# Fox attention: sums turned before they are inverted, raw output turned a unit later, copies begun at another unit

## The chip, the cores and the metric

One NeuronCore of a Trainium2 chip runs the whole program. The metric is the device time of one execution in microseconds (us), lower is better. Only one of the program's stages is touched by the change.

## What is computed

One layer of a hybrid decoder over a prompt of 2048 tokens and 8 sequences of 8 new tokens, all in float32: an input projection, two kinds of attention (8 heads each), an output projection and a squared-ReLU MLP. The stage that the change touches is the prompt's part of the first kind, the forgetting attention ("fox"):

```python
def block(args):                      # one block of 128 queries, 8 heads of 64 dims
    s = einsum('bqhd,bkhd->bhqk', qi, k) * scale
    s = s + ci[..., :, None] - c_k[..., None, :]     # c: running sum of log-forget values
    s = where(kpos[None, :] <= qpos[:, None], s, NEG_INF)
    p = softmax(s, axis=-1)
    return einsum('bhqk,bkhd->bqhd', p, v)
```

A further output of the layer is the window buffer of 8 decode sequences (new_win_k): the old buffer (win_k) shifted by 8 rows. It needs no arithmetic and is copied from memory to memory by DMA while the fox stage runs.

## The kernel before

The program is a row of phases with a barrier of all engines between them: projection, fox attention, dilated attention, the decode samples, and the output projection with the MLP in two halves. `attend_fox` is one phase.

**Tiling.** Heads go in four pairs (p); the 2048 queries in four macros (m) of 512 columns. A *unit* G is two key tiles of 128 keys against one macro, for both heads z of the pair: four score tiles of 128 keys x 512 queries. Causality gives macro m 2(m+1) units, so 20 units a pair (u counts them: 0-1, 2-5, 6-11, 12-19) and 80 in all. `last_unit(n)` is the last unit of macro n = 4p + m (u = 1, 5, 11, 19), and `ended(G - k)` names the macro, if any, that ended k units ago.

**The work of one unit.**
- TensorE writes the transposed scores into one of three PSUM banks `s_ps` (`scores`, L1153, L1154, the mask L1156 on the diagonal). ScalarE turns each into exponentials `pT` in SBUF (L1043); `pT` has room for four units. TensorE multiplies `pT` by the values into `o_ps` (`values`, L1170), for two units at a time, in odd G. GpSimd adds the exponentials up over the key tiles in `acc` (L1002, L1006).
- Beside this, for macros and head pairs that come later, TensorE computes the plain scores once more into one of two PSUM banks `low_ps` (`low_scores`, L1123, L1126), and VectorE takes each row's maximum with the decay added (`largest`, L1062). These "lows" give the number that is subtracted in the softmax. `fox_plan` spreads them over the units, some four to seven in most; after unit 9 of the last pair there are none left. TensorE may start low number o only when VectorE has finished low o - 2: there are two banks.
- When a macro's maxima are there, TensorE transposes them (`turn_max`, L1133) into the shared PSUM bank `x_ps`, and VectorE copies them into `qb` (`take_off`, L1075). This falls in units u = 1, 5, 11 of pair 0, and u = 14, 17 (for the next pair), 4 and 11 after that.

**The end of a macro.** Two units after its last one, TensorE sums `acc` over the partitions with a matrix of ones, so that every one of a head's 64 rows of `x_ps` holds the same sum (`denominators`, L1179). VectorE inverts all 128 x 512 of them and multiplies `o_ps` by the result into `o_f` (`post`, L1082 and L1086). Three units after, TensorE transposes `o_f` into `x_ps` (`turn_back`, L1186), ScalarE copies that into `o_sb` (L1019) and sends it to memory (L1023).

**What sets the order.** Each engine runs its own list in program order: an instruction that waits holds up all that stand behind it. `x_ps` is one bank with several users; `x_uses` lists them in TensorE's order, and `take_x` makes TensorE wait until the one before has been read. In a step G TensorE does: scores with the lows between them, values (odd G), denominators, turn_max, turn_back. VectorE does: lows, post, take_off. ScalarE does: at u = 0 and 10 the issue of a copy of 4080 KB for new_win_k (L1032; eight in all, for G = 0, 10, ... 70), the four exponentials, then fetch_back.

**Loads.** SyncE's queue loads the first pair's data quarter by quarter (x = 0 to 3): q (three DMAs of 256 KB, L898, L899), ka (two, L908), decay (one of 512 KB, L922), kb (one, L912), v (two of 128 KB, L917). The first low needs q and ka of x = 0, VectorE's part of it the decay, the first score kb as well. The loads for the next pair follow through the stage, behind waits on `scored`, `maxed` and `pv`; the last of them, q of macro 3, is issued when unit 19's scores are done and is first needed by the lows of u = 3.

Of the kernel before, what the change touches and what calls it, by code (L numbers as in the profile page):

```python
# [13 lines left out]
ALU = mybir.AluOpType  # L14
# [4 lines left out]
P = 128  # L19
# [6 lines left out]
HD = 64  # L26
# [752 lines left out]
def attend_fox(nc, c, dram):  # L779
# [10 lines left out]
    with Phase(nc, "fox") as ph:  # L790
# [11 lines left out]
        neg_c = ph.sb("neg_c", [P, TILES, HEADS])  # L802
        rden = ph.sb("rden", [P, Q_COLS])
        o_f = ph.sb("o_f", [P, 2, Q_COLS])
# [26 lines left out]
        added = ph.sem("added")  # L831
        den_done = ph.sem("den_done")
        inverted = ph.sem("inverted")
        posted = ph.sem("posted")
        o_turned = ph.sem("o_turned")
        returned = ph.sem("returned")
        o_sent = ph.sems("o_sent")
# [15 lines left out]
        def ended(G):  # L853

            return [n for n in range(HEAD_PAIRS * MACROS) if last_unit(n) == G]
# [15 lines left out]
        def x_uses():  # L871

            uses, count = [], dict(den=0, turn=0, back=0)
            def use(kind):
                count[kind] += 1
                uses.append((kind, count[kind]))
            use("turn")
            for G in range(UNITS + 3):
                for _n in ended(G - 2):
                    use("den")  # L880
                for _x in planned(G, "turn"):
                    use("turn")
                for _n in ended(G - 3):
                    use("back")
            return uses
# [5 lines left out]
        def _(sp):  # L891
# [42 lines left out]

            for x in range(MACROS):
                load_q(0, x)
                load_ka(0, x)
                load_decay(0, x)
                load_kb(0, x)
                load_v(0, x)  # L940
            sp.dma_start(table[:, :], dram["page_table"]).then_inc(table_loaded, 16)
# [72 lines left out]
        def _(act):  # L1014
            def fetch_back(n):
                act.wait_ge(o_turned, n + 1)
                if n >= 2:
                    act.wait_ge(o_sent[n % 2], 16 * (n // 2))
                act.activation(o_sb[:, n % 2, :, :], x_ps[:, :].rearrange("p (j d) -> p j d", d=P), ACT.Copy)\  # L1019
                    .then_inc(returned, 1)  # L1020
                act.wait_ge(returned, n + 1)
                p, m = divmod(n, MACROS)
                act.dma_start(dram["att"][m * Q_COLS:(m + 1) * Q_COLS, p * P:(p + 1) * P]  # L1023
                              .rearrange("(j p) d -> p j d", p=P), o_sb[:, n % 2, :, :]).then_inc(o_sent[n % 2], 16)

            act.wait_ge(decay_set, 1)
            for G in range(UNITS + 3):
                if G < UNITS:
                    p, u, m, kt = unit(G)
                    if u % 10 == 0:  # L1030
                        b = G // 10
# [6 lines left out]
                    for k in range(2):  # L1038
                        x = reach(kt + k, m)
                        for z in range(2):  # L1040
# [3 lines left out]
                                           bias=neg_c[:, kt + k, 2 * p + z:2 * p + z + 1]).then_inc(exped, 1)  # L1044
                for n in ended(G - 3):
                    fetch_back(n)
            act.dma_start(dram["new_win_k"][:, PAST - DEC_SEQ:PAST, :],
# [7 lines left out]
        def _(dve):  # L1055
# [15 lines left out]
            def take_off(p, m):  # L1071
                dve.wait_ge(m_turned, turn_order.index((p, m)) + 1)
                if p > 0:
                    dve.wait_ge(scored, 4 * (last_unit(MACROS * (p - 1) + m) + 1))
                dve.tensor_copy(qb[HD:HD + 2, :, m, :], x_ps[0:2, :].unsqueeze(1).to_broadcast([2, 2, Q_COLS]))\  # L1075
                    .then_inc(m_set, 1)

            def post(n):
                dve.wait_ge(den_done, n + 1)
                if n > 0:  # L1080
                    dve.wait_ge(posted, n)
                dve.reciprocal(rden[:, :], x_ps[:, :]).then_inc(inverted, 1)  # L1082
                dve.wait_ge(inverted, n + 1)
                if n >= 2:
                    dve.wait_ge(o_turned, n - 1)
                dve.tensor_tensor(o_f[:, n % 2, :], o_ps[n % 2][:, :], rden[:, :], ALU.mult).then_inc(posted, 1)  # L1086

# [5 lines left out]
            take_off(0, 0)  # L1093
            for G in range(UNITS + 2):
                for todo in planned(G, "low"):
                    largest(*todo)
                for n in ended(G - 2):
                    post(n)
                for todo in planned(G, "turn"):
                    take_off(*todo)  # L1100

        @block.tensor
        def _(pe):
# [5 lines left out]
            def take_x():  # L1109

                k = next(x_count)
                if k > 0:
                    kind, count = uses[k - 1]
                    pe.wait_ge(inverted if kind == "den" else m_set if kind == "turn" else returned, count)

# [43 lines left out]
            def values(G):  # L1159
# [4 lines left out]
                if kt == 0 and n >= 2:  # L1164
                    pe.wait_ge(posted, n - 1)
                pe.wait_ge(exped, 4 * (G + 1))
# [8 lines left out]
            def denominators(n):  # L1175
# [4 lines left out]
                mm.then_inc(den_done, 1)  # L1180

            def turn_back(n):
                take_x()
                pe.wait_ge(posted, n + 1)
                for j in range(MACRO):
# [11 lines left out]
            pe.wait_ge(decay_set, 1)  # L1197
            for G in range(UNITS + 3):
                todo = planned(G, "low")
# [11 lines left out]
                for x in planned(G, "turn"):  # L1211
                    turn_max(*x)
                for n in ended(G - 3):
                    turn_back(n)

# [1607 lines left out]
```

## Time and profile before

| what | us |
|---|---|
| median of 3 runs (lowest to highest) | 3939.76 (3939.62 to 3942.84) |
| the profiled execution, its own time | 3937.29 |
| its span, first to last instruction | 3935.6 |
| of which the fox phase, first load issued to last DMA issued | 694.4 to 1268.2 |
| first score to last score | 729.7 to 1252.6 |
| granted TensorE clock, mean of the span | 0.945 of 2.4 GHz |

The profile is one execution. Times in its rows are us from the span's start. A timeline row has start, duration, engine, line and operation, and in brackets how long the engine was idle before it and whose result ended that. A row of a view by windows has the stretch, its length, the busy time of each engine with the number of instructions, the granted TensorE clock (1.00 is 2.4 GHz, 0.50 is 1.2 GHz), the share of the DMA engines' time and GB/s.

### The profile page before, as it was taken

To read this page: it belongs to the slowest core of one execution; us is meant where nothing else is said; L and a number is where in the kernel's file an instruction comes from. 1 tells how busy PE (TensorE), PEld (TensorE's weight loads), DVE (VectorE), ACT (ScalarE), POOL (GpSimd) and SP (SyncE) were. 2 spreads that over 40 slices of the span, in tenths; PEclk is the share of its full clock that TensorE was granted. 3 is DMA by queue.
4 is the path that set the end of the run, shared out by engine and by line. 5 is a ranking of instruction groups with operands and counts; after the bars stand their busy time and mean duration, and the time that the engine had idled before them with its cause. 6 is when DMAs were issued, how large, how long until landed. Compare 5 with 4: busy or idle time off the path is not lost. (4 is left out here: it accounts for less than half of the span.)

```text
span 3935.6 us, 48805 instructions
## 1 busy us (share of the span) xinstructions
PE 3574.1 (91%) x17899; PEld 2793.2 (71%) x17944; DVE 1522.4 (39%) x2977; ACT 1022.4 (26%) x1484; POOL 945.7 (24%) x838
## 2 busy tenths in 40 slices
PE   8999998588887699988997989999998899999999
PEld 7987786344443477774443768888886788888888
DVE  2223333455552455534332333434433233333333
ACT  3322222143333133332222322111212321111111
POOL 2223466265556011120133110000000200000010
PEclk9999999698888699999999989999998999999999
DMA  5546666855542755628986311111114021111111
GB/s 195 193 163 203 224 203 197 179 149 134 162 113 80 186 161 169 167 78 326 341 308 191 122 58 61 43 43 52 54 32 161 24 70 44 43 43 43 43 43 59
DMA packets 301411, 507.52 MB, mean 129 GB/s; under 512 B 64146, under 2 KB 197780, under 8 KB 292756
## 3 DMA queue, kind: packets, MB, share of 16 engines
q1 hardware_dynamic: 272692, 374.48, 31.7%
q10 hardware_dynamic: 14584, 75.85, 5.5%
q0 software_dynamic: 13952, 54.80, 3.8%
q8 instruction: 109, 1.79, 0.2%
q14 instruction: 74, 0.61, 0.1%
HBM read 408.18 MB, written 164.50 MB: 146 GB/s over the span
## 5 line engine op out<-in xcount | busy, mean ns | idle before, releaser
L2619 DVE TENSOR_TENSOR fin_x<-mlp_y,fin_x 128x512 f32<-128x512 f32 x544 | 350.0, 685 | 747.0 <-PE mlp_y L2662 747.0
L2639 PE MATMUL mlp_u<-fin_h_hi,mlp_w_hi 128*128 128x512 f32 (+2 forms) x1280 | 451.6, 353 | 29.2 <-DVE mlp_w_lo L2595 29.2
L2641 PE MATMUL mlp_u<-fin_h_hi,mlp_w_lo 128*128 128x512 f32 (+2 forms) x1280 | 451.3, 353 | 0.0
L2640 PE MATMUL mlp_u<-fin_h_lo,mlp_w_hi 128*128 128x512 f32 (+2 forms) x1280 | 451.2, 352 | 0.0
L2579 POOL TENSOR_TENSOR mlp_u<-mlp_r 128x1024 f32<-128x1024 f32 (+2 forms) x80 | 131.7, 1646 | 1329.4 <-ACT mlp_r L2520 1329.4
L2660 PE MATMUL mlp_y<-mlp_w_hi,mlp_u_hi 128*128 128x512 f32 x1088 | 423.8, 389 | 0.9 <-DVE fin_x L2619 0.9
L2661 PE MATMUL mlp_y<-mlp_w_lo,mlp_u_hi 128*128 128x512 f32 x1088 | 424.3, 390 | 0.0
L2662 PE MATMUL mlp_y<-mlp_w_hi,mlp_u_lo 128*128 128x512 f32 x1088 | 423.9, 390 | 0.0
L667 PE MATMUL proj_z<-proj_w_hi,proj_x_hi 128*128 128x512 f32 (+1 forms) x816 | 312.2, 383 | 26.9 <-DMA proj_x_lo<-scratch_xt 12.7
L669 PE MATMUL proj_z<-proj_w_hi,proj_x_lo 128*128 128x512 f32 (+1 forms) x816 | 306.3, 375 | 0.0
L668 PE MATMUL proj_z<-proj_w_lo,proj_x_hi 128*128 128x512 f32 (+1 forms) x816 | 306.0, 375 | 0.0
L1006 POOL TENSOR_TENSOR fox_acc<-fox_acc,fox_pT 128x512 f32<-128x512 f32 (+3 forms) x256 | 269.3, 1079 | 130.7 <-ACT fox_pT L1043 126.1
L1043 ACT ACTIVATE fox_pT<-fox_s,fox_neg_c 128x512 f32<-128x512 f32 (+3 forms) x320 | 190.3, 625 | 347.1 <-PE fox_s L1154 190.8
L2639 PEld LDWEIGHTS mlp_u<-fin_h_hi,mlp_w_hi 128*128 128x128 f32 x1280 | 241.5, 189 | 52.9 <-DVE mlp_w_lo L2595 30.0
L1062 DVE CUSTOM_DVE_ANT_0 fox_low<-fox_low,fox_decay 128x512 f32<-128x512 f32 (+3 forms) x320 | 191.9, 610 | 175.2 <-PE fox_low L1123 78.5
L2640 PEld LDWEIGHTS mlp_u<-fin_h_lo,mlp_w_hi 128*128 128x128 f32 x1280 | 241.5, 189 | 22.0
L2641 PEld LDWEIGHTS mlp_u<-fin_h_hi,mlp_w_lo 128*128 128x128 f32 x1280 | 241.4, 189 | 20.2
L2520 ACT ACTIVATE mlp_r<-mlp_u 128x1024 f32<-128x1024 f32 (+2 forms) x80 | 69.9, 874 | 706.5 <-PE mlp_u L2641 706.5
L1461 DVE CUSTOM_DVE_ANT_0 dil_low<-dil_low,dil_allowed 128x512 f32<-128x512 f32 (+2 forms) x320 | 185.0, 609 | 161.4 <-PE dil_low L1525 124.4
L2662 PEld LDWEIGHTS mlp_y<-mlp_w_hi,mlp_u_lo 128*128 128x128 f32 x1088 | 200.8, 185 | 46.4
L2660 PEld LDWEIGHTS mlp_y<-mlp_w_hi,mlp_u_hi 128*128 128x128 f32 x1088 | 200.8, 185 | 45.4 <-DVE fin_x L2619 1.3
L2661 PEld LDWEIGHTS mlp_y<-mlp_w_lo,mlp_u_hi 128*128 128x128 f32 x1088 | 200.8, 185 | 44.7
(236 smaller groups left out, 6160.4 us busy)
## 6 DMA issues: line engine op xcount, KB each, us to landing
samp_k_in<-in_cache_k SPq DMA_DIRECT2D x128, 256.0 KB, 4.7
samp_v_in<-in_cache_v POOLq DMA_DIRECT2D x128, 256.0 KB, 4.8
mlp_w_raw<-in_w_up SPq DMA_DIRECT2D x64, 512.0 KB, 4.5
mlp_w_raw<-in_w_down SPq DMA_DIRECT2D x64, 512.0 KB, 4.4
out_new_win_k<-in_win_k ACTq DMA_DIRECT2D x8, 4080.0 KB
out_new_win_v<-in_win_v ACTq DMA_DIRECT2D x8, 4080.0 KB
proj_x_hi<-scratch_xt SPq DMA_DIRECT2D x34, 512.0 KB, 6.3
proj_x_lo<-scratch_xt SPq DMA_DIRECT2D x34, 512.0 KB, 6.3
```

What stands on the lines that cost most here:

```text
L667: pe.matmul(out, x_hi[:, slot, xs], w_hi[:, p % 2, ws], start=(k == 0), stop=False)
L668: pe.matmul(out, x_hi[:, slot, xs], w_lo[:, p % 2, ws], start=False, stop=False)
L669: mm = pe.matmul(out, x_lo[:, slot, xs], w_hi[:, p % 2, ws], start=False, stop=(k == KC - 1))
L1006: op = pool.tensor_tensor(to[:, x:Q_COLS], to[:, x:Q_COLS], tiles[k][z][:, x:Q_COLS], ALU.add)
L1062: dve.tensor_tensor_reduce(low[:, o % 2, 0:n], low_ps[o % 2][:, 0:n], decay[:, z, x, 0:n], 1.0, -3e38, ALU.add, ALU.max, piece_max[:, p % ...
L2619: dve.tensor_tensor(part, y_ps[(tiles * par + t) % 2][0:rows, q * D_G:(q + 1) * D_G], part, ALU.add).then_inc(y_added, 1)
L2639: pe.matmul(out, hi, h_hi[:, k, c0:c0 + n], start=(k == 0), stop=False)
L2640: pe.matmul(out, hi, h_lo[:, k, c0:c0 + n], start=False, stop=False)
L2641: mm = pe.matmul(out, lo, h_hi[:, k, c0:c0 + n], start=False, stop=(k == KC - 1))
L2660: pe.matmul(out, hi, w_hi[:, par, 2 + f, b_], start=(f == 0), stop=False)
L2661: pe.matmul(out, hi, w_lo[:, par, 2 + f, b_], start=False, stop=False)
L2662: mm = pe.matmul(out, lo, w_hi[:, par, 2 + f, b_], start=False, stop=(f == FB - 1))
```

## The change

- The sums are no longer inverted where they stand. ScalarE copies 65 rows of them (one row of each head is among these) from `x_ps` to SBUF (`fetch_sums`), TensorE transposes these 65 rows (`turn_sums`, four transposes, three units after the macro's end), and VectorE inverts only the 128 x 8 numbers that matter (`invert`).
- ScalarE copies the output undivided from `o_ps` to `o_f` (`fetch_output`), TensorE transposes it four units after the macro's end (`turn_back`), and VectorE multiplies it by the inverted sums on its way from `x_ps` to `o_sb` (`post`). ScalarE then only issues the DMA (`send`, five units after).
- `x_ps` has one more use a macro. VectorE's order in a step becomes: lows, take_off, invert, post.
- The copies for new_win_k are issued at u = 5 and 15 in place of 0 and 10.
- The first pair's loads go ka before q, and kb and v of a quarter behind the ka, q and decay of the next.

```diff
@@ -800,7 +800,8 @@
         piece_max = ph.sb("piece_max", [P, 2, N_LOW])
         nm = ph.sb("nm", [P, 2, MACROS, MACRO, 2])
         neg_c = ph.sb("neg_c", [P, TILES, HEADS])
-        rden = ph.sb("rden", [P, Q_COLS])
+        den = ph.sb("den", [HD + 1, 2, Q_COLS])
+        rden = ph.sb("rden", [P, 2, MACRO, 2])
         o_f = ph.sb("o_f", [P, 2, Q_COLS])
         o_sb = ph.sb("o_sb", [P, 2, MACRO, P])
         ident_bf = ph.sb("ident_bf", [P, P], BF16)
@@ -870,17 +873,19 @@
 
         def x_uses():
 
-            uses, count = [], dict(den=0, turn=0, back=0)
+            uses, count = [], dict(den=0, turn=0, across=0, back=0)
             def use(kind):
                 count[kind] += 1
                 uses.append((kind, count[kind]))
             use("turn")
-            for G in range(UNITS + 3):
+            for G in range(UNITS + 5):
                 for _n in ended(G - 2):
                     use("den")
                 for _x in planned(G, "turn"):
                     use("turn")
                 for _n in ended(G - 3):
+                    use("across")
+                for _n in ended(G - 4):
                     use("back")
             return uses
 
@@ -933,11 +938,14 @@
                 sp.wait_ge(scored, 4 * (NU_FOX * p + u + 1))
 
             for x in range(MACROS):
+                load_ka(0, x)
                 load_q(0, x)
-                load_ka(0, x)
                 load_decay(0, x)
-                load_kb(0, x)
-                load_v(0, x)
+                if x > 0:
+                    load_kb(0, x - 1)
+                    load_v(0, x - 1)
+            load_kb(0, MACROS - 1)
+            load_v(0, MACROS - 1)
             sp.dma_start(table[:, :], dram["page_table"]).then_inc(table_loaded, 16)
             sp.wait_ge(table_loaded, 16)
             for p in range(HEAD_PAIRS - 1):
@@ -1012,22 +1020,29 @@
 
         @block.scalar
         def _(act):
-            def fetch_back(n):
-                act.wait_ge(o_turned, n + 1)
+            def fetch_sums(n):
+                act.wait_ge(den_done, n + 1)
                 if n >= 2:
-                    act.wait_ge(o_sent[n % 2], 16 * (n // 2))
-                act.activation(o_sb[:, n % 2, :, :], x_ps[:, :].rearrange("p (j d) -> p j d", d=P), ACT.Copy)\
-                    .then_inc(returned, 1)
-                act.wait_ge(returned, n + 1)
+                    act.wait_ge(den_turned, n - 1)
+                act.activation(den[:, n % 2, :], x_ps[0:HD + 1, :], ACT.Copy).then_inc(den_out, 1)
+
+            def fetch_output(n):
+                act.wait_ge(pv, last_unit(n) + 1)
+                if n >= 2:
+                    act.wait_ge(o_turned, n - 1)
+                act.activation(o_f[:, n % 2, :], o_ps[n % 2][:, :], ACT.Copy).then_inc(o_out, 1)
+
+            def send(n):
+                act.wait_ge(posted, n + 1)
                 p, m = divmod(n, MACROS)
                 act.dma_start(dram["att"][m * Q_COLS:(m + 1) * Q_COLS, p * P:(p + 1) * P]
                               .rearrange("(j p) d -> p j d", p=P), o_sb[:, n % 2, :, :]).then_inc(o_sent[n % 2], 16)
 
             act.wait_ge(decay_set, 1)
-            for G in range(UNITS + 3):
+            for G in range(UNITS + 6):
                 if G < UNITS:
                     p, u, m, kt = unit(G)
-                    if u % 10 == 0:
+                    if u % 10 == 5:
                         b = G // 10
                         act.dma_start(dram["new_win_k"][b:b + 1, 0:PAST - DEC_SEQ, :].rearrange("b t d -> (b t) d"),
                                       dram["win_k"][b:b + 1, DEC_SEQ:PAST, :].rearrange("b t d -> (b t) d"))\
@@ -1042,8 +1057,11 @@
                             act.wait_ge(scored, n + 1)
                             act.activation(pT[:, n % PT_N, x:Q_COLS], s_ps[n % S_BANKS][:, x:Q_COLS], ACT.Exp,
                                            bias=neg_c[:, kt + k, 2 * p + z:2 * p + z + 1]).then_inc(exped, 1)
-                for n in ended(G - 3):
-                    fetch_back(n)
+                for n in ended(G - 2):
+                    fetch_output(n)
+                    fetch_sums(n)
+                for n in ended(G - 5):
+                    send(n)
             act.dma_start(dram["new_win_k"][:, PAST - DEC_SEQ:PAST, :],
                           dram["k_b"][SEQ:SEQ + N_SAMPLE, :].rearrange("(b q) d -> b q d", q=DEC_SEQ))\
                 .then_inc(moved, 16)
@@ -1075,15 +1093,20 @@
                 dve.tensor_copy(qb[HD:HD + 2, :, m, :], x_ps[0:2, :].unsqueeze(1).to_broadcast([2, 2, Q_COLS]))\
                     .then_inc(m_set, 1)
 
+            def invert(n):
+                dve.wait_ge(den_turned, n + 1)
+                dve.reciprocal(rden[:, n % 2, :, :], x_ps[:, 0:MACRO * (HD + 1)].rearrange("p (j c) -> p j c", j=MACRO)
+                               [:, :, 0:HD + 1:HD]).then_inc(inverted, 1)
+
             def post(n):
-                dve.wait_ge(den_done, n + 1)
-                if n > 0:
-                    dve.wait_ge(posted, n)
-                dve.reciprocal(rden[:, :], x_ps[:, :]).then_inc(inverted, 1)
                 dve.wait_ge(inverted, n + 1)
+                dve.wait_ge(o_turned, n + 1)
                 if n >= 2:
-                    dve.wait_ge(o_turned, n - 1)
-                dve.tensor_tensor(o_f[:, n % 2, :], o_ps[n % 2][:, :], rden[:, :], ALU.mult).then_inc(posted, 1)
+                    dve.wait_ge(o_sent[n % 2], 16 * (n // 2))
+                dve.tensor_tensor(o_sb[:, n % 2, :, :].rearrange("p j (z d) -> p j z d", z=2),
+                                  x_ps[:, :].rearrange("p (j z d) -> p j z d", j=MACRO, z=2),
+                                  rden[:, n % 2, :, :].unsqueeze(3).to_broadcast([P, MACRO, 2, HD]), ALU.mult)\
+                    .then_inc(posted, 1)
 
             dve.wait_ge(summed, 1)
             dve.tensor_scalar(neg_c[:, :, :].rearrange("p t h -> p (t h)"), s_ps[0][:, 0:TILES * HEADS], -1.0, None,
@@ -1091,13 +1114,15 @@
             for o in range(LOW_BASE[1]):
                 largest(0, o)
             take_off(0, 0)
-            for G in range(UNITS + 2):
+            for G in range(UNITS + 5):
                 for todo in planned(G, "low"):
                     largest(*todo)
-                for n in ended(G - 2):
-                    post(n)
                 for todo in planned(G, "turn"):
                     take_off(*todo)
+                for n in ended(G - 3):
+                    invert(n)
+                for n in ended(G - 4):
+                    post(n)
 
         @block.tensor
         def _(pe):
@@ -1111,7 +1136,8 @@
                 k = next(x_count)
                 if k > 0:
                     kind, count = uses[k - 1]
-                    pe.wait_ge(inverted if kind == "den" else m_set if kind == "turn" else returned, count)
+                    pe.wait_ge(den_out if kind == "den" else m_set if kind == "turn" else
+                               inverted if kind == "across" else posted, count)
 
             def low_scores(p, o):
                 m, x, j, z = LOW_ORDER[o]
@@ -1162,7 +1188,7 @@
                 if kt % MACRO == 0:
                     pe.wait_ge(v_loaded[kt // MACRO], 32 * (p + 1))
                 if kt == 0 and n >= 2:
-                    pe.wait_ge(posted, n - 1)
+                    pe.wait_ge(o_out, n - 1)
                 pe.wait_ge(exped, 4 * (G + 1))
                 for k in range(2):
                     x = reach(kt + k, m)
@@ -1179,9 +1205,17 @@
                     mm = pe.matmul(x_ps[half(z), :], c["ones"][:, 0:HD], acc[:, n % 2, z, :], start=True, stop=True)
                 mm.then_inc(den_done, 1)
 
+            def turn_sums(n):
+                take_x()
+                pe.wait_ge(den_out, n + 1)
+                for j in range(MACRO):
+                    mm = pe.transpose(x_ps[:, j * (HD + 1):(j + 1) * (HD + 1)], den[:, n % 2, j * P:(j + 1) * P],
+                                      c["ident"][0:HD + 1, 0:HD + 1])
+                mm.then_inc(den_turned, 1)
+
             def turn_back(n):
                 take_x()
-                pe.wait_ge(posted, n + 1)
+                pe.wait_ge(o_out, n + 1)
                 for j in range(MACRO):
                     mm = pe.transpose(x_ps[:, j * P:(j + 1) * P], o_f[:, n % 2, j * P:(j + 1) * P], c["ident"][:, :])
                 mm.then_inc(o_turned, 1)
@@ -1195,7 +1229,7 @@
                 low_scores(0, o)
             turn_max(0, 0)
             pe.wait_ge(decay_set, 1)
-            for G in range(UNITS + 3):
+            for G in range(UNITS + 5):
                 todo = planned(G, "low")
                 for k in range(4):
                     if G < UNITS:
@@ -1211,6 +1245,8 @@
                 for x in planned(G, "turn"):
                     turn_max(*x)
                 for n in ended(G - 3):
+                    turn_sums(n)
+                for n in ended(G - 4):
                     turn_back(n)
 
 
```

## Rows read from the trace of the kernel before

**Rows 1.** The page: the span, and TensorE's busy time (share) and instructions.
```profile
span 3935.6 us, 48805 instructions
...
PE 3574.1 (91%) x17899; PEld 2793.2 (71%) x17944; DVE 1522.4 (39%) x2977; ACT 1022.4 (26%) x1484; POOL 945.7 (24%) x838
```
**Rows 2.** By windows: the fox stage's main stretch and its end.
```profile
748.00:1218.00 470.00, 400.57 (x1816) 226.58 (x1812) 256.22 (x649) 176.48 (x294) 270.92 (x258) 0.89 0.51 137
...
1218.00:1260.00 42.00, 35.98 (x154) 17.04 (x156) 4.81 (x3) 18.57 (x33) 34.14 (x31) 0.92 0.02 7
```
**Rows 3.** Waits of PE, 748 to 1218: total us, times, longest.
```profile
PE fox_low L1123 <- DVE fox_piece_max L1062: 46.3, 41, 3.3
PE fox_x L1186 <- DVE fox_qb L1075: 8.3, 6, 1.7
PE fox_low L1123 <- DMA fox_qb<-scratch_zt: 7.0, 3, 3.6
PE fox_s L1153 <- issue: 6.8, 5, 1.4
```
**Rows 4.** Timeline of PE, units 14 and 15 of pair 0.
```profile
842.03 0.47 PE L1123 MATMUL fox_low<-fox_ka,fox_qa 128*128 128x512 f32 x1 [2.82 <-DVE fox_piece_max L1062]
...
846.13 1.11 PE L1186 MATMUL fox_x<-all_ident,fox_o_f 128*128 128x128 f32 x4 [1.31 <-DVE fox_qb L1075]
846.90 0.78 PE L1153 MATMUL fox_s<-fox_qa,fox_ka 128*128 128x512 f32 x1
```
**Rows 5.** Timeline of DVE at the same place.
```profile
837.19 3.36 DVE L1082 RECIPROCAL fox_rden<-fox_x 128x512 f32<-128x512 f32 x1 [2.58 <-PE fox_x L1179]
840.59 0.69 DVE L1086 TENSOR_TENSOR fox_o_f<-fox_o,fox_rden 128x512 f32<-128x512 f32 x1
```
**Rows 6.** By windows: two stretches of low clock, and the sum of the 13 behind a post.
```profile
843.00:851.00 8.00, 6.30 (x26) 4.29 (x25) 3.49 (x13) 2.67 (x5) 3.09 (x3) 0.57 0.11 33
...
sum 103.00, PE 86.55 PEld 57.95 DVE 46.73 ACT 28.51 POOL 39.22; mean PE 6.66 PEld 4.46 DVE 3.59 ACT 2.19 POOL 3.02
...
1154.00:1161.00 7.00, 5.92 (x15) 3.97 (x17) 3.24 (x9) 2.07 (x3) 3.61 (x4) 0.52 0.29 64
```
**Rows 7.** Timeline of the stage's start: ACT's queue, PE and DVE.
```profile
696.00 0.70 ACTq L1032 DMA_DIRECT2D out_new_win_k<-in_win_k  x1
...
718.17 0.45 PE L1123 MATMUL fox_low<-fox_ka,fox_qa 128*128 128x128 f32 x1 [22.53 <-DMA fox_ka<-scratch_zt]
...
720.92 0.29 DVE L1062 CUSTOM_DVE_ANT_0 fox_low<-fox_low,fox_decay 128x128 f32<-128x128 f32 x1 [24.95 <-DMA fox_decay<-scratch_negc]
...
729.71 0.77 PE L1153 MATMUL fox_s<-fox_qa,fox_ka 128*128 128x512 f32 x1 [1.46 <-issue]
```
**Rows 8.** DMA queues, 700 to 706: packets, MB, share (q10 ACT's, q1 SP's).
```profile
q10 hardware_dynamic: 37, 2.42, 103.6%
q1 hardware_dynamic: 109, 0.19, 11.0%
```
**Rows 9.** By windows: SP's loads alone on the DMA engines.
```profile
730.00:740.00 10.00, 8.86 (x25) 5.57 (x25) 5.54 (x18) 2.54 (x4) 2.58 (x4) 0.50 1.13 189
```
**Rows 10.** Timeline of SP's queue: q of macro 3 behind a copy.
```profile
875.26 10.43 SPq L898 DMA_DIRECT2D fox_qa<-scratch_zt  x2
```
**Rows 11.** Timeline of PE: four small transposes and what follows.
```profile
865.69 0.60 PE L1133 MATMUL fox_x<-all_ident,fox_nm 128*2 128x128 f32 x4
866.05 0.48 PE L1153 MATMUL fox_s<-fox_qa,fox_ka 128*128 128x512 f32 x1
```
**Rows 12.** Timeline of the stage's end.
```profile
1259.88 1.87 PE L1179 MATMUL fox_x<-fox_acc,all_ones 128*64 128x512 f32 x4 [2.89 <-POOLq L1011]
1261.79 3.36 DVE L1082 RECIPROCAL fox_rden<-fox_x 128x512 f32<-128x512 f32 x1 [30.80 <-PE fox_x L1179]
...
1266.02 1.09 PE L1186 MATMUL fox_x<-all_ident,fox_o_f 128*128 128x128 f32 x4 [4.27 <-DVE fox_o_f L1086]
1267.14 0.60 ACT L1019 ACTIVATE fox_o_sb<-fox_x 128x512 f32<-128x512 f32 x1 [13.77 <-PE fox_x L1186]
```

More of the change, by code:

```diff
@@ L832, in attend_fox @@
         den_done = ph.sem("den_done")
+        den_out = ph.sem("den_out")
+        den_turned = ph.sem("den_turned")
+        o_out = ph.sem("o_out")
         inverted = ph.sem("inverted")
@@ L835, in attend_fox @@
         o_turned = ph.sem("o_turned")
-        returned = ph.sem("returned")
         o_sent = ph.sems("o_sent")
```

## The prediction

> **What bounds the kernel now.** I began with the page: TensorE is busy 91% of the span and everything else under 40% [rows 1], so a gain has to shorten TensorE's line of work, by taking out idle time or by giving it its full clock. Only the fox stage is touched, so the next view is its windows. From 748 to 1218 TensorE is busy 400.6 of 470 us, at a mean clock of 0.89 [rows 2]. That is 69 us idle, and 2 x 0.11 x 470 = 103 us spent at 1.2 GHz in place of 2.4.
>
> The waits say what ends the idle time [rows 3]. Lows waiting for VectorE are 46.3 us in 41 waits. In the timeline 14 of these are 2.46 to 3.27 us long, 38.5 us together, and each stands behind one of the 14 reciprocals of this stretch; the 27 others share 7.8 us. One of the 14 is the 2.82 at 842.03 [rows 4]. VectorE at that place [rows 5]: it takes the sums at 837.19, inverts for 3.36, multiplies for 0.69, and only then gets to the lows. TensorE fills its two banks of lows and stands. VectorE's 4.05 us cost 2.82, so about 1.2 us of VectorE work at this point are free. The six waits of L1186 for take_off and the five before L1153 (8.3 and 6.8 us) are waits for VectorE's copy of the maxima, the three on a DMA (7.0) are lows of macro 3 whose q is late.
>
> Behind the long waits the clock is down: 843 to 851 at a mean 0.57, which is 6.9 us at 1.2 GHz. I asked for the 13 stretches of low clock that follow a post; 103 us of windows, 86.55 of them busy [rows 6], and by their own clocks 92.6 us at 1.2 GHz.
>
> The start is bound by loads. The first low stands until 718.17, VectorE's first until 720.92, the first score is at 729.71 [rows 7], while the phase's first load is issued at 694.4. A copy issued at 696.00 [rows 7] moves 2.42 MB between 700 and 706, and the loads beside it 0.19 MB [rows 8].
>
> **The change, part by part**, against the profiled execution's 3937.3 us. The median shown is 2.5 above that, which I add at the end.
>
> *VectorE's inversion.* It removes 3.36 us for each macro and adds an inversion of 128 x 8, for which there is no row: more than the 0.08 of an accumulator read and less than 3.36; I take 0.2, by its 8 columns against 512. The multiplication stays at 0.69 [rows 5]. The two are now in different steps, and each is under the 1.2 us that are free, with or without take_off ahead of the inversion (take_off delays TensorE itself, before and after). So the 14 long waits go: **38.5 us**, bounds 30 (a remainder of 0.6 each) and 38.5.
>
> *Clock.* If TensorE is never again at 1.2 GHz behind these posts, 92.6 us, 84% busy, run in half the time: 39 us. The two stretches behind DMA waits (the 7 us at 0.52 are one, [rows 6]) give 4.5 more. Upper end 43. Six of the stretches hold a wait for take_off too (58.5 of the 92.6 us); if these all stay low, 25 are not gained: 19 is left. At full clock the lows also run up against VectorE's pace: the 27 short waits are that. I take **26**, 60% of the upper end, and 12 as the lower.
>
> *Start.* Now ka, q and decay of x = 0 come first with no copy beside them. The loads alone ran at 189 GB/s [rows 9]. With 2 us before bytes move (my estimate, 0 to 4), ka and q (1.31 MB) are there at 694.4 + 2 + 6.9 = 703.3 and the decay (0.52 MB) at 706.1. From VectorE's first low to the first score were 8.8 us, so that path gives 714.9. But kb now stands behind the ka, q and decay of x = 1: 3.93 MB, 20.8 us, so 717.2. The later one sets the start: 12.5 us earlier than 729.71. I take **12**, bounds 4 (a slower queue) and 15. The loads behind it (v of x = 0 at about 719, x = 2 by 731, x = 3 by 742) are each ahead of their first use, which moves to about 735, 738 and 752.
>
> *Copies at u = 5 and 15.* The number and size are the same. Now a copy at u = 0 is in flight when q of macro 3 is issued: its two first DMAs hold SP's queue 10.43 us [rows 10], and the lows that need it wait 7.0 us in all. A copy at u = 15 should be over by u = 19, though SP's queue, with ka, kb and v behind it, may run some 5 us late. The cover for these is slack: they are needed in the next pair. At u = 5 it is q of macro 1 and the decays, needed at u = 11. If that slack is gone the cost is the copy itself (last rival). **7.0**, bounds 0 and 7. The eighth copy, at G = 75, is hidden by the five units behind it.
>
> *Added on TensorE.* Four transposes of 65 rows a macro. Four of 2 columns at full clock took 865.69 to 866.05, 0.36 us [rows 11]; four of 128 at half clock 0.77 [rows 4]. By the nearer, 16 x 0.36 = **5.8**, upper bound 12.3. At pair ends (three times) turn_back stands directly behind the next macro's sums, and `take_x` waits for ScalarE's copy, 0.60 [rows 12] and two handovers: 3 x 1.0 = **3.0**, bounds 0 and 6.
>
> *Added on ScalarE.* One copy more a macro. Behind the waits of `fetch_output` and `fetch_sums` stand the exponentials of the next unit. They need scores that TensorE only computes after the sums, so the delay is about 0.6 less the 0.5 of a score, and three score banks and four units of `pT` hide it from TensorE and GpSimd. Nothing, at most 16 x 0.6 = 10. The DMA of the output a step later holds only `o_sb`, which has a second buffer: nothing.
>
> *The end.* From 1218 GpSimd's sums bound the tail: 34.1 busy of 42 [rows 2], and TensorE waits 2.89 for them [rows 12]. What TensorE gains there is mostly lost; I take 2.0, between nothing and half of the 7.9 idle. The last chain goes from 1261.79 to 1267.74, 5.95 us [rows 12]; the new one is 0.60 + 1.09 + 0.2 + 1.09 + 0.69 and 0.5 of handovers, 4.2: **1.8** less.
>
> Sum: 12 + 38.5 + 7.0 + 26 + 2.0 + 1.8 - 5.8 - 3.0 = 78.5. 3937.3 - 78.5 = 3858.8, and 2.5 above that 3861.3: **3861 us**.
>
> **The rivals.**
>
> *The clock stays down (0.20).* In units 4 and 14 the order is now four transposes, the wait of 1.31 for take_off, four more transposes. For it: the clock is low across 843 to 851, with just this pattern in it [rows 4, 6]. Against: there it had been brought down by the 2.82 before. Then only 12 of the 26 come: 3875. If five waits more bring it down, at 2.9 us each, 3889. The Trainium skill (TensorE: Matmul & The Clock Gate, Part 4: PE-mode transpose) says that transposes don't count as activity for the clock as multiplications do; by that rule this is the likelier case. The trace has no long run of transposes that would test it.
>
> *The start and the q of macro 3 are not gained (0.12).* SP's queue stalls with more loads of 256 KB ahead of kb, or runs late behind the copy at u = 15. For it: the 10.43 us in one issue [rows 10]. 8 + 7 back: 3876.
>
> *The one bank passes too slowly (0.10).* Sums, ScalarE, transposes, VectorE, transposes, VectorE: two more handovers a macro, and ScalarE's copy behind a late sum. At 1.25 us for each of 16 macros: 3881. Against: all but the three at pair ends are a unit apart.
>
> *Copies in the wrong place (0.03): slower.* At u = 5 and 15 a copy holds up loads that TensorE wants at once. Place: the decays and q of macro 1, and kb and v of the next pair. A copy moved 2.42 MB in 6 us, so 4.18 MB take 10.4; if TensorE stood for all of it eight times, and lost 2.9 at low clock behind each, 106 us: 3967. It decides from 78.5 / 8 = 9.8 us a copy. Against: five units or more lie before the first use.
>
> *It doesn't do what it says (0.02).* The lows wait for something else that only coincides with the reciprocal: about 3939.
>
> **How the numbers follow.** The forecast has 0.53, the rivals 0.20, 0.12, 0.10, 0.03 and 0.02. Its own range is 3842 (clock 43, tail full) to 3875. Reaching to the dearer rivals gives 3842 to 3892. A measurement of this kernel tells 0.2%, some 8 us, from no change; all but the last two cases are beyond that: faster 0.95, same 0.02, slower 0.03.
>
> **What would show it.** Right: no reciprocal of 3.36; in the waits of PE, L1123 on VectorE's maxima at about 8 us for 30 waits; the DMA wait of L1123 gone; the first score near 717; the clock of the main stretch at 0.95 or more; the last transposes some 78 us earlier than 1266. Wrong: L1123 waits of over 1 us at the posts, `take_x` waits on ScalarE at more than the three pair ends, a clock near 0.89 with the idle time gone, a first score later than 725, or a DMA that a low or a score waits for in units 5 to 11 or 15 to 19.

## The result, and the profile after

| | before | after |
|---|---|---|
| median, us (lowest to highest, 4 runs each) | 3939.69 (3935.18 to 3942.84) | 3848.93 (3845.03 to 3857.08) |
| ratio, 95% interval | | 0.9773 (0.9754 to 0.9792) |
| profiled execution, own time | 3937.29 | 3845.03 |
| mean granted clock of the span | 0.945 | 0.962 |

The change takes 90.8 us off the median; 78.5 were forecast, and 3848.93 lies in the range. The page shows the 64 matmul records of the added transposes, and fewer busy us on TensorE for them (before: [rows 1]):

```profile
span 3843.4 us, 48967 instructions
...
PE 3529.3 (92%) x17963; PEld 2765.4 (72%) x18008; DVE 1473.9 (38%) x2977; ACT 1031.6 (27%) x1500; POOL 946.0 (25%) x838
```

The two profiles are best laid side by side from the fox phase's first load, since the projection ahead of it ended 4.9 us earlier in the profile of after (first load at 689.5 against 694.4; it ranges from 689 to 695 over the profiles below, whatever the kernel). By windows, in three parts: first load to first score, to the last score, to the next phase's first load. Before, then after:

```profile
694.40:729.70 35.30, 7.56 (x24) 4.58 (x25) 5.57 (x19) 0.00 (x0) 4.42 (x4) 0.50 0.91 227
729.70:1252.60 522.90, 449.20 (x1994) 252.38 (x1995) 270.40 (x684) 198.49 (x333) 303.37 (x288) 0.87 0.50 130
1252.60:1272.30 19.70, 7.35 (x36) 2.81 (x35) 4.05 (x2) 1.38 (x4) 6.64 (x8) 0.69 0.07 20
```
```profile
689.50:715.90 26.40, 7.57 (x24) 4.58 (x24) 5.58 (x19) 0.00 (x0) 4.42 (x4) 0.50 0.88 183
715.90:1158.00 442.10, 409.90 (x2054) 229.70 (x2054) 224.83 (x684) 207.17 (x348) 300.00 (x286) 0.98 0.60 161
1158.00:1178.60 20.60, 8.28 (x41) 3.54 (x39) 0.90 (x2) 2.09 (x5) 9.85 (x12) 0.73 0.06 19
```

The phase is 577.9 us before and 489.1 after, 88.8 less: 8.9 at the start, 80.8 in the main part, and 0.9 more at the end. In the main part TensorE's idle time falls from 73.7 to 32.2 us (41.5 less), and its busy time from 449.2 to 409.9 (39.3 less) although it has more to do. That second half is the clock: 0.98 in place of 0.87. Not all of it lies behind the posts. From the first score on, the clock stays at 1.2 GHz for 18.3 us before, and for 4.3 us after:

```profile
729.70:748.00 18.30, 17.16 (x54) 10.78 (x56) 9.37 (x33) 4.22 (x8) 4.95 (x8) 0.50 1.13 186
```
```profile
715.90:720.20 4.30, 4.23 (x10) 2.38 (x10) 1.61 (x5) 1.37 (x2) 0.49 (x2) 0.50 1.04 219
```

The waits of PE in the main part (total, times, longest) answer to [rows 3]:

```profile
PE fox_low L1149 <- DVE fox_piece_max L1080: 12.0, 40, 0.6
PE fox_x L1212 <- DVE fox_qb L1093: 9.1, 6, 1.7
PE fox_s L1179 <- issue: 6.8, 5, 1.4
PE fox_s L1179 <- DMA fox_kb<-scratch_zt: 5.3, 1, 5.3
...
PE fox_x L1220 <- ACT fox_den L1027: 2.1, 3, 0.7
PE fox_x L1220 <- DVE fox_qb L1093: 1.3, 1, 1.3
```

The long waits of the lows are gone (longest 0.6), the DMA wait of the lows too. Left are take_off (L1093), the kb of the very first score, and the three pair ends where TensorE waits for ScalarE's copy of the sums. The last chain in the timeline of the phase's end answers to [rows 12], and shows each new piece with its duration:

```profile
1168.51 1.98 PE L1205 MATMUL fox_x<-fox_acc,all_ones 128*64 128x512 f32 x4 [5.99 <-POOLq L1019]
1170.52 0.59 ACT L1027 ACTIVATE fox_den<-fox_x 65x512 f32<-65x512 f32 x1 [7.36 <-PE fox_x L1205]
...
1171.96 0.21 DVE L1098 RECIPROCAL fox_rden<-fox_x 128x8 f32<-128x8 f32 x1 [24.63 <-PE fox_x L1212]
...
1173.44 0.69 DVE L1106 TENSOR_TENSOR fox_o_sb<-fox_x,fox_rden 128x512 f32<-128x512 f32 x1 [1.27 <-PE fox_x L1220]
1174.16 0.37 ACTq L1038 DMA_DIRECT2D scratch_att<-fox_o_sb  x1
```

From the end of the sums to the send it is 3.7 us in place of 6.0. But TensorE now stands 5.99 us for GpSimd's sums where it stood 2.89: at the end GpSimd is the bound, and TensorE's gain there turns into this wait.

### The profile page after: what moved, and what is told of

Same layout as the page of the kernel before. It is cut to its first block and busy times, and to the rows that moved or that the text cites. A ratio compares the mean times of both kernels' runs of the same rounds, so it can differ in the third digit from the quotient of the medians.

```text
span 3843.4 us, 48967 instructions
## 1 busy us (share of the span) xinstructions
PE 3529.3 (92%) x17963; PEld 2765.4 (72%) x18008; DVE 1473.9 (38%) x2977; ACT 1031.6 (27%) x1500; POOL 946.0 (25%) x838
```

## The experiments

Each kernel was run beside the kernel before on the same chip, and the ratio is to that one (its medians lie between 3938.50 and 3941.08). "Phase" is the fox phase's length in the profile, first load to the next phase's first load, which leaves the scatter of the rest out (behind the phase the rest takes 2661 to 2674 us over the profiles, whatever the kernel). It is one execution's figure, and that execution's own time can lie far from its kernel's median: 10 us above it for e6, 8 for e3, 7 below it for e12. The median holds everything.

| run | median us | ratio (95% interval) | phase us |
|---|---|---|---|
| before | 3939.69 | | 577.9 |
| after | 3848.93 | 0.9773 (0.9754 to 0.9792) | 489.1 |
| e1 copies back | 3888.39 | 0.9870 (0.9849 to 0.9891) | 523.5 |
| e2 load order back | 3851.81 | 0.9781 (0.9761 to 0.9801) | 486.2 |
| e3 both back | 3885.17 | 0.9861 (0.9843 to 0.9879) | 534.0 |
| e4 before, no inversion | 3898.27 | 0.9883 (0.9856 to 0.9910) | 533.0 |
| e5 loads and copies only | 3923.30 | 0.9958 (0.9944 to 0.9972) | 554.4 |
| e6 dose of 0.9 us | 3860.60 | 0.9793 (0.9776 to 0.9809) | 501.7 |
| e7 dose of 1.7 us | 3878.53 | 0.9839 (0.9823 to 0.9855) | 518.3 |
| e8 dose of 3.4 us | 3907.40 | 0.9921 (0.9904 to 0.9937) | 542.7 |
| e0 after, again | 3852.28 | 0.9777 (0.9761 to 0.9794) | 489.0 |
| e9 sums first | 3838.11 | 0.9746 (0.9728 to 0.9763) | 477.3 |
| e10 and kb first | 3835.19 | 0.9740 (0.9723 to 0.9757) | 477.8 |
| e12 and turn at 10 | 3826.91 | 0.9717 (0.9702 to 0.9731) | 468.3 |

### What each part brings: e1, e2, e3, e5

e1, in the kernel after:

```diff
-                    if u % 10 == 5:
+                    if u % 10 == 0:
```

> The kernel after, with only the copies put back to u = 0 and 10. My theory (the 3.4 us inversion and the clock behind it carry most of the gain, the copies some 20 us of it): the copy is back among the first loads and holds the DMA engines some 10 us, so the first score comes about 36 us after the phase's first load in place of 26; q of macro 3 is late again in three pairs, 7 us and some low clock behind it. 3849 + 10 + 7 + 4 = about 3870. The rival (the copies' place is the main part of the gain, because they hold up loads all through the stage): 3890 or more, with DMA waits of TensorE of over 20 us. If the load order alone cures the start: about 3860.

e2, in the kernel after, the first pair's loads as before:

```diff
-                load_ka(0, x)
                 load_q(0, x)
+                load_ka(0, x)
                 load_decay(0, x)
-                if x > 0:
-                    load_kb(0, x - 1)
-                    load_v(0, x - 1)
-            load_kb(0, MACROS - 1)
-            load_v(0, MACROS - 1)
+                load_kb(0, x)
+                load_v(0, x)
```

> The kernel after, with only the first pair's loads in the old order (q, ka, decay, kb, v for each quarter). My theory: in the kernel after the first score waits 5.3 us for kb, which the new order put behind the next quarter; with the old order that wait is gone, ka comes a little later, and the first score stands about 21 to 22 us after the first load in place of 26.4: 3844 to 3849. The rival (the new order is what brings the start forward): first score after 30 us or more, 3853 to 3858.

e3 has both edits.

> The kernel after, with the copies at u = 0 and 10 and the loads in the old order: only the change of the sums and of the output's path is left. My theory: start as in the kernel before (35.3 us to the first score, so 9 us back), 7 us of late q and 4 of clock: about 3869, that is some 70 of the 91 us come from this part alone. The rival (copies and loads do most): nearer to 3939 than to 3849.

e1 came to 3888, nearer to its rival than to my theory: the copies' place is worth 39.5 us with the new arithmetic (34.4 by the phases, and 33.4 by the medians of e3 and e2, where the loads are in the old order). The start is 12.5 us later (38.9 us to the first score), and the waits of PE in e1 have 16.7 us in 3 waits for the late q of macro 3 where the kernel before had 7.0 [rows 3]. The rival's DMA waits of over 20 us are there only if the 4.7 for kb at the first score are counted, which the kernel after has too (5.3). e3 came to 3885, 16 above my 3869, and has 19.6 us of waits for q. PE's waits in e3:

```profile
PE fox_low L1146 <- DMA fox_qb<-scratch_zt: 19.6, 3, 7.3
PE fox_low L1146 <- DVE fox_piece_max L1077: 11.0, 35, 0.7
```

and SyncE's queue there, behind the copy that ScalarE's queue issued at 853.90, with TensorE's low that waits for it:

```profile
857.76 11.03 SPq L903 DMA_DIRECT2D fox_qa<-scratch_zt  x2
```
```profile
876.14 0.79 PE L1146 MATMUL fox_low<-fox_ka,fox_qa 128*128 128x512 f32 x1 [6.12 <-DMA fox_qb<-scratch_zt]
```

SyncE is held as long as before (10.43, [rows 10]); what changed is TensorE. In the kernel before it gets to the low that needs this q 15.2 to 16.1 us after SyncE began to issue it (three pairs), in e3 after 11.4 to 12.7; the low starts 17.5 to 18.8 us after the issue before, 17.7 to 20.0 in e3. Held up behind the posts, TensorE used to come late to that load as well. Rid of them it comes earlier and stands longer. So the old inversion hid part of what the copies cost. e5 tests that from the other side: the kernel before with the copies and load order of after.

> The kernel before, with only the copies at u = 5 and 15 and the new load order; the arithmetic as before. Theory now: the late q of macro 3 cost only 7.0 us in the kernel before because TensorE, held up at each post, came late to it as well; without those holds the same lateness cost 16.7 to 19.6 us (first and third run). So moved alone, the loads and copies bring 9 at the start, 7 of waits and some 5 of clock: 3941 - 21 = about 3920, and the two parts add to less than the whole (21 + 56 against 91). The rival (the parts simply add): 3941 - (91 - 56) = 3906.

3923, as forecast (3920), and not the 3906 of parts that add. By phases: the arithmetic alone takes off 43.9 us (e3), loads and copies alone 23.5 (e5), together 88.8; 21.4 come only from having both. By the ratios it is 55, 17 and 89, so 18. The longer waits for q are 12.6 of it; the rest was not taken apart.

e2's first score stands 22.3 us behind the first load, as expected, against 26.4 after: the new load order makes the start later, not earlier. Its phase is 2.8 shorter and its median 2.9 longer than after's, so the order itself is worth nothing that these runs can tell. 3852 lies between my 3844 to 3849 and the rival's 3853 to 3858.

### What the inversion costs by itself: e4, e6, e7, e8

e4, in the kernel before:

```diff
-                dve.reciprocal(rden[:, :], x_ps[:, :]).then_inc(inverted, 1)
+                dve.tensor_copy(rden[:, :], x_ps[:, :]).then_inc(inverted, 1)
```

> The kernel before, with a copy of 128x512 in place of the reciprocal; the output is left undivided by its sum (multiplied by it). VectorE's work behind a macro falls from 4.05 to about 1.4 us, nothing is added to TensorE or ScalarE. My theory: the long waits shrink to about 0.2 us, the clock returns, and against the arithmetic-only kernel it saves the added transposes and handovers (6 to 9 us): 3860 to 3866. The rival (it was where the inversion and the multiplication stand in the queues, two in one step, not how long the inversion takes, that cost the time): over 3890, with long waits of L1123 left.

No wait of L1123 on VectorE is longer than 0.6 us in it, so the rival's ground is gone: how long VectorE is held is what counts, not where. The shorter hold alone takes 44.9 us off the phase. But the time was 3898, not 3860 to 3866. I had again taken 7 us for the late q; it is 17.0 in this kernel, and the rest of the miss stays open. The phase is e3's within 1 us (533.0 and 534.0; the 10.4 us that e4's profile is longer otherwise lie behind the phase). That is no proof that the added transposes, copies and handovers are free: e4 had 81 us at 1.2 GHz in its main part and e3 73, which would hide some 4 us.

e6 to e8 put VectorE's hold back into the kernel after by steps; here e8, with 128 and 256 columns in e6 and e7:

```diff
             def invert(n):
                 dve.wait_ge(den_turned, n + 1)
+                dve.reciprocal(spare[:, 1, 0:512], spare[:, 0, 0:512]).then_inc(spare_done, 1)
+                dve.wait_ge(spare_done, n + 1)
```

> The kernel after, with one more reciprocal of 128x128 on a private tile ahead of each small inversion, about 0.9 us of VectorE work a macro. By the prediction 1.2 us of VectorE work at this point are free (4.05 us cost a wait of 2.82): 0.2 + 0.9 stays under it, so no new long waits of L1149 and the same time, 3849 within 4. The rival (no slack: VectorE's lows follow closely): 14 x 0.9 = 13 us more, 3862.

> The same with 128x256, about 1.7 us. By the slack of 1.2, waits of about 0.7 us behind each of some 14 macros: 10 us. If waits this short leave the clock up: about 3859. The rival, that these too bring the clock down: 10 + 14 x 2.5 = 45, so 3890.

> The same with 128x512, 3.36 us: VectorE's old hold is back in the new arrangement, everything else as after. Waits of about 2.3 us at some 14 places, 33 us, and the clock down behind most of them; the profiles of before and after give about 45 us for the clock's return in all. My theory: 33 + 30 to 40, so 3912 to 3922. The rival (the clock's return came from the loads and the steadier order, not from these waits): 33 us and little more, about 3882, with a clock in the main stretch still over 0.95.

The waits of L1156 on VectorE in the stage (total, times, longest) in e6 and e8; after had 12.0:

```profile
PE fox_low L1156 <- DVE fox_piece_max L1083: 16.6, 45, 1.0
```
```profile
PE fox_low L1156 <- DVE fox_piece_max L1083: 40.3, 42, 3.4
```

e8: 28.3 us more waiting, and the phase is 53.6 longer. Some 3.4 of the other 25 us are the last macro's own dose, in the chain at the end. The rest is the clock: with the same matmuls TensorE is busy for 432.5 us in the main part, some 22 more than in after, and the main part has 21 us at 1.2 GHz in after and 83 in e8. e8's main part, and then the clock's mean in the same stretch (after, e8):

```profile
720.79:1213.81 493.02, 432.50 (x2056) 240.26 (x2056) 272.82 (x699) 207.08 (x349) 299.91 (x286) 0.92 0.55 145
```

```profile
740.00:1120.00 380.00, 353.33 (x1793) 198.83 (x1792) 204.84 (x628) 177.29 (x294) 260.15 (x248) 0.98 0.60 163
```
```profile
740.00:1160.00 420.00, 367.04 (x1760) 204.65 (x1761) 245.87 (x634) 174.83 (x292) 253.85 (x242) 0.92 0.56 149
```

3907 is 5 us under my 3912 to 3922 and 25 above the rival's 3882. So the rival, that the clock's return had another source, falls. The waits of e8 that are new and long are 11, of 1.87 to 3.42 us; the clock is down behind all but the first (2.69 at 761.44), and together they cost themselves and about four fifths as much again at 1.2 GHz. e7's 10.9 us of added waits, none over 1.8, cost 29.2 of phase, between my two cases: short waits bring the clock down in some places and not in others.

e6 missed: 3861, where the rival has 3862 and I had 3849 within 4. The time alone doesn't decide it, as 14 of the 18 us that its profile has more at 1.2 GHz stand ahead of the first dose, at the stage's start. Its waits do: they grew by 4.6 us, a third of what no slack would give, but four of them, 0.77 to 1.01 us long, stand where after has none over 0.4. With the dose VectorE's work there is 1.2 us. So the free 1.2 us are not there behind every macro.

### Beating both: e0, e9, e10, e12

In after, the three falls of the clock in the main part (867 to 874, 979 to 983, 1088 to 1096) each follow the same place, u = 4 of pairs 1 to 3: four transposes of the maxima, 1.71 us of waiting for take_off, four transposes of the sums. (In the profile of e0, the same kernel again, it is u = 4 of pairs 2 and 3, and u = 14 of pair 2, where the wait is 1.31.) e9 turns the order of the two round, on TensorE, on VectorE and in the list of users; TensorE's part:

```diff
-                for x in planned(G, "turn"):
-                    turn_max(*x)
                 for n in ended(G - 3):
                     turn_sums(n)
+                for x in planned(G, "turn"):
+                    turn_max(*x)
```

> The kernel after, unchanged, so that the three below have it on the same chip: 3849, between 3845 and 3857. If its single runs differ, the clock in the main stretch differs with them: stretches at 1.2 GHz of some 3.4 us or twice that, in other places or another number.

> The kernel after, with the turned sums ahead of the turned maxima in a step, on TensorE and VectorE. Where both fall in one step (u = 4 and 14), TensorE now waits for the small inversion (0.2 us) and not for take_off (1.2 us). My theory: in the kernel after six waits of 1.31 to 1.71 us of the turned sums (9.1 us in all) bring the clock down at the three places at u = 4. They shrink to some 0.4 us: 6 us less, and the clock stays up there, 8 us less: about 3836. By the Trainium skill (TensorE: Matmul & The Clock Gate, Part 4: PE-mode transpose) transposes don't count as activity; by that rule the eight transposes in a row, which stay, would bring the clock down as before, and only the 6 us come: 3843.

3838 against 3852 for after on the same chip, where I had 3836. The six waits of 9.1 us became six of 3.4. After's timeline at u = 4 of pair 1 and its clock, then e9's:

```profile
866.95 0.69 PE L1212 MATMUL fox_x<-all_ident,fox_den 65*128 65x65 f32 x4 [1.71 <-DVE fox_qb L1093]
```
```profile
867.00:874.00 7.00, 7.00 (x26) 4.25 (x28) 1.61 (x5) 1.68 (x4) 2.87 (x5) 0.52 1.04 384
```
```profile
868.95 0.41 PE L1212 MATMUL fox_x<-all_ident,fox_den 65*128 65x65 f32 x4
870.13 0.60 PE L1159 MATMUL fox_x<-all_ident,fox_nm 128*2 128x128 f32 x4 [0.78 <-DVE fox_rden L1098]
```
```profile
740.00:1120.00 380.00, 356.69 (x1851) 201.94 (x1850) 209.32 (x643) 182.88 (x306) 269.14 (x256) 1.00 0.62 165
870.00:877.00 7.00, 6.87 (x41) 4.01 (x42) 3.07 (x7) 1.49 (x4) 4.13 (x6) 1.00 1.09 368
```

The eight transposes in a row are still there, with 0.78 us between the two fours, and the clock stays at 1.00 in both windows. One such pair of rows proves little, because the kernel after does not always fall there either. In e0, at this very place and at u = 14 of pair 2:

```profile
871.00:878.00 7.00, 6.78 (x41) 3.99 (x42) 2.18 (x7) 1.49 (x4) 3.07 (x5) 1.00 1.23 421
1038.00:1045.00 7.00, 7.00 (x24) 4.55 (x24) 2.51 (x10) 2.75 (x4) 5.01 (x5) 0.52 0.85 298
```

But over all of these places, six in a profile (u = 4 and 14), the clock fell behind 6 of 12 in after and e0, and behind none of 18 in e9, e10 and e12. So it is the length of the wait that brings it down, and the transposes alone don't. Whether a wait as long would do it without transposes on both sides is not shown. The Trainium skill (TensorE: Matmul & The Clock Gate, Part 4: PE-mode transpose) says that transposes don't count as busy for the clock in the way that multiplications do; in this pattern that made no difference that a row shows, and no run here has a long stretch of them.

e10 adds one edit to the loads, so that kb of x = 0 comes behind its decay:

```diff
                 load_decay(0, x)
-                if x > 0:
+                if x == 0:
+                    load_kb(0, 0)
+                if x > 1:
                     load_kb(0, x - 1)
+                if x > 0:
                     load_v(0, x - 1)
```

> The one before, and the first pair's kb of x = 0 loaded right behind its decay. In the kernel after the first score waits 5.3 us for this load. My theory: it stands 21 to 22 us behind the phase's first load in place of 26.4, and nothing behind it is late: 5 us less than the one before, about 3831. The rival: the loads of x = 1 to 3 are the limit soon after, and the 5 us are waited for there: 3836.

The first score came 22.6 us behind the first load, 3.3 earlier than in e9, and the phase is as long as e9's. No wait for a load is left in its main part, so the rival's ground isn't there, though the time (3835) is the rival's 3836. The clock was at 1.2 GHz for 10 us between 724 and 738, where e9, once up, stayed up until 1124: the stage began earlier and slower. The medians differ by 2.9 us with intervals that overlap: open.

e12 adds a change in the plan:

```diff
-            spans, turns = [(-9, -8), (-7, -5), (-4, 2), (3, 9)], [-6, -3, 4, 11]
+            spans, turns = [(-9, -8), (-7, -5), (-4, 2), (3, 9)], [-6, -3, 4, 10]
```

> The one before, and the maxima of macro 3 turned at u = 10 in place of 11 for pairs 1 to 3. Unit 12's first score then no longer waits for take_off: three waits of 1.35 us (named issue in the waits of PE) go, 4 us, and a fall of the clock behind them if there was one: about 3827. The rival: at u = 10 the maxima are not reduced yet, and TensorE waits there instead: 3831 or more.

3826.9, its interval (0.9702 to 0.9731) clear of after's on the same chip (0.9761 to 0.9794): 25 us faster than the kernel after and 112 faster than before, the best of all. The waits named issue went from 8.2 us in 6 in e10 to 4.2 in 3 (one of these at the first score), and the main part has 3.5 us at 1.2 GHz. The step from e10 alone is 8 us, where I had 4, and the two intervals still touch.

## Why the prediction was right

By the steps of the prediction, against the fox phase of the profile (78.5 forecast, 88.8 measured):

- **VectorE's inversion: right.** 38.5 forecast; the lows' waits on VectorE in the main part went from 47.5 to 12.0, 35.5 less, and a wait of 2.0 for `o_f` at 1231.13 besides. The small inversion takes 0.21, taken as 0.2. The free 1.2 us per post are not there behind every macro (e6); the change itself needs less, as it puts its 0.21 and 0.69 into different steps.
- **Clock: mechanism right, size off.** 26 were taken, 60% of an upper end of 43. TensorE's busy time in the main part fell by 39.3 with 16 groups of transposes more in it (3.5, below), so the clock gave some 43. Some 6 of these belong to the first 18 us after the first score, for which the prediction has no term; they come with the loads and copies, since e5, with the old inversion, is also up after 4.0 us. About 37 are left for 26 taken (an estimate from the rows). The step that was mis-sized is the discount. I let six stretches stay down because a wait for take_off lies in them, and held the lows to VectorE's pace. In after the wait of 1.31 at u = 14 brought the clock down nowhere, that of 1.71 at u = 4 three times (in e0 once and twice), and the lows' short waits went from 9.0 us in 29 to 12.0 in 40, 0.3 each as before. The first rival (the clock stays down) happened at three of its places and cost about 8 us: 17 us at 1.2 GHz, nearly all busy.
- **Start: right in kind, 8.9 for 12.** The first score waited for kb, as worked out, but 26.4 us in and not 22.8. 4.84 MB had moved by then, not 3.93: the loads issued behind kb move beside it.
- **Copies: right for the pair, and too small as a cause.** 7.0 of waits went to none, as forecast. What the prediction missed is that the wait is not a constant: with the new arithmetic and the old copies it is 16.7 to 19.6 us (e1, e3). The start and this wait, with the clock behind it, make the copies' move worth 33 to 40 us and not 20.
- **Added work: less than taken.** 5.8 were taken for the transposes by the nearest row of four with 128 columns; with 65 columns a group takes 0.22 us to the next score (1035.97 to 1036.19 in e8), so 3.5. The three pair ends cost 2.1 for 3.0. The waits for take_off, taken as unchanged, went from 8.3 us in 6 to 10.4 in 7. ScalarE's copies cost nothing seen.
- **End: right in its parts.** From the first score of unit 12 to the sums it is 38.8 us after and 41.0 before, and the last chain 3.7 and 6.0, so 4.6 for 3.8. The window of the end alone looks 0.9 longer because its start, the last score, moved ahead of GpSimd.

The bank `x_ps` did not pass too slowly, the copies held up nothing at u = 5 and 15, and the reciprocal was the cause of the long waits (e4, e8). The rest of the program is 3.4 us shorter in the profile of after (4.9 in the projection, -1.5 behind the phase); the projection's part is scatter by the range above.

## What to carry to other kernels

Where one engine is the bound and stands for another a few us at a time, ask how its clock goes in the stretch behind each stand, and count that as a term of its own: here it was as large as the waits. A transfer's lateness is a time, not a cost: when the stands ahead of it go, the same late load is waited for longer, so move it together with them. And when an operation repeats one number across 64 rows, turn the sums first and invert the few that differ, 0.21 us for 3.36.

## What the runs showed of the hardware that was not expected

- Single runs scatter as their clock does. Five runs of the same kernel (e0) lie between 3844.5 and 3856.5, at mean clocks from 0.961 to 0.957, lowest clock with longest time.
- Whether a short wait brings the clock down is not the same from one execution to the next. In the two profiles of the kernel after (after and e0), a wait of 1.71 us between two groups of four transposes was followed by a fall within 2.5 us in five of six places, one of 1.31 in one of eight. The place at u = 4 of pair 1 fell in one and not in the other, with the same waits in front of it.
- A load on a queue does not have the DMA engines to itself until it is done: kb, issued at 702.2, landed about 14 us later while 256 and 512 KB loads issued behind it moved too.
